# Layer norms of a two-layer decoder: sums by matmul onto every partition, a reciprocal root with a Newton step, and another order of the token parts

## The reference

```python
ALPHA = (2.0 * DEPTH) ** 0.25
def layer_norm(x, g, b):
    mu = jnp.mean(x, axis=-1, keepdims=True)
    var = jnp.mean(jnp.square(x - mu), axis=-1, keepdims=True)
    return (x - mu) * lax.rsqrt(var + EPS) * g + b

for l in range(DEPTH):
    x = layer_norm(ALPHA * x + 0.5 * swiglu(x, ffn1_w_in[l], ffn1_w_out[l]), ...)
    x = layer_norm(ALPHA * x + hybrid_mixer(x, ...), ...)      # RG-LRU | gated linear attention | convolution
    x = layer_norm(ALPHA * x + memory_cross_attn(x, mem, ...), ...)
    x = layer_norm(ALPHA * x + 0.5 * swiglu(x, ffn2_w_in[l], ffn2_w_out[l]), ...)
```

## Time and profile before

| | |
|---|---|
| median of 3 runs | 2443.06 us (2442.2 to 2444.05) |
| profiled execution | 2449.32 us, span 2447.5 us |
| mean granted TensorE clock | 0.959 |
| TensorE busy | 2310.8 us, 94% of the span |
| VectorE, ScalarE, GpSimd busy | 45%, 33%, 42% |
| HBM traffic | 211.5 MB, 86 GB/s |

### The profile page before, as it was taken

One profiled execution on the slowest core, in us unless ns is written; L12 is line 12 of the kernel. 1 busy time (PEld: TensorE's weight loads), 2 busy tenths in 40 slices (PEclk: granted clock), 3 DMA queues, 4 the chain that ended last, 5 costly groups with the idle time before them and its releaser, 6 DMA issues.

```text
span 2447.5 us, 26512 instructions
## 1 busy us (share of the span) xinstructions
PE 2310.8 (94%) x10912; PEld 1920.0 (78%) x10912; DVE 1111.5 (45%) x1179; ACT 797.6 (33%) x1079; POOL 1031.1 (42%) x430
## 2 busy tenths in 40 slices
PE   7999998969999899999999999989799998999997
PEld 6888887856878788888788888877568877888886
DVE  2333325886644533332333332359866454333333
ACT  3322224524444422222233222145345434222222
POOL 5444444423462444444344444343245624444441
PEclk9999998978999899999899999999789998999998
DMA  4223221211341132332122232212113411322321
GB/s 166 95 95 107 101 85 61 86 38 56 97 133 54 55 103 95 99 113 95 64 87 95 95 108 98 79 61 78 48 60 100 129 53 62 101 96 95 112 95 35
DMA packets 55721, 213.24 MB, mean 87 GB/s; under 512 B 6064, under 2 KB 8368, under 8 KB 55344
## 3 DMA queue, kind: packets, MB, share of 16 engines
q1 hardware_dynamic: 54304, 207.64, 25.5%
q10 hardware_dynamic: 1296, 3.90, 0.4%
HBM read 209.42 MB, written 2.10 MB: 86 GB/s over the span
## 4 chain that ended last, share of the span: by engine, by line
PE 82%; DVE 9%; ACT 3%; ACTq 1%; POOL 1%; DVEq 1%; issue 1%; DMA 0%; SPq 0%
PE psum L457 23%; PE psum L458 23%; PE psum L461 23%; DVE tmp L1520 4%; POOL w_lo L380 1%; PE psum L588 1%; PE psum L493 1%; ACT x L1048 1%; PE psum L664 1%; PE psum L620 1%; PE psum L665 1%; ACTq L1062 1%; ACT act_hi L1063 1%; PE psum L670 1%; ACT w_hi L1011 1%
## 5 line engine op out<-in xcount | busy, mean ns | idle before, releaser
L380 POOL TENSOR_TENSOR w_lo<-raw,w_hi 128x1024 fp32r<-128x1024 f32 (+2 forms) x360 | 945.6, 2629 | 1307.8 <-ACT w_hi L1011 1307.7
L1011 ACT ACTIVATE w_hi<-raw 128x1024 fp32r<-128x1024 f32 (+2 forms) x360 | 405.2, 1126 | 1362.5 <-PE psum L461 1237.5
L457 PE MATMUL psum<-act_hi,w_hi 128*128 128x512 f32 x1836 | 728.3, 397 | 36.2 <-ACT w_hi L1011 36.2
L458 PE MATMUL psum<-act_lo,w_hi 128*128 128x512 f32 x1836 | 724.0, 394 | 0.0
L461 PE MATMUL psum<-act_hi,w_lo 128*128 128x512 f32 x1836 | 454.0, 389 | 0.0
L457 PEld LDWEIGHTS psum<-act_hi,w_hi 128*128 128x128 f32 x1836 | 351.0, 191 | 115.9 <-issue 35.5
L458 PEld LDWEIGHTS psum<-act_lo,w_hi 128*128 128x128 f32 x1836 | 350.8, 191 | 73.8 <-issue 0.5
L461 PEld LDWEIGHTS psum<-act_hi,w_lo 128*128 128x128 f32 x1836 | 344.7, 188 | 72.1
L1436 DVE TENSOR_TENSOR work<-work,psum 128x512 f32<-128x512 f32 x88 | 60.5, 688 | 609.5 <-PE psum L461 562.2
L457 PE MATMUL psum<-h_hi,w_hi 128*128 128x512 f32 x616 | 243.3, 395 | 0.0
L458 PE MATMUL psum<-h_lo,w_hi 128*128 128x512 f32 x616 | 243.3, 395 | 0.0
(11 more groups left out here) (246 smaller groups left out, 2410.9 us busy)
## 6 DMA issues: line engine op xcount, KB each, us to landing
raw<-w_in SPq DMA_DIRECT2D x176, 512.0 KB, 3.5
raw<-w_out SPq DMA_DIRECT2D x64, 704.0 KB, 4.0
raw<-w_mix SPq DMA_DIRECT2D x36, 512.0 KB, 3.5
raw<-w_kv SPq DMA_DIRECT2D x32, 512.0 KB, 3.5
raw<-w_mixout SPq DMA_DIRECT2D x16, 576.0 KB, 3.7
raw<-w_q SPq DMA_DIRECT2D x16, 512.0 KB, 3.5
raw<-w_o SPq DMA_DIRECT2D x16, 512.0 KB, 3.5
raw<-w_v SPq DMA_DIRECT2D x4, 768.0 KB, 4.1
```

The costliest lines, as they stand in the source:

```text
L380: nc.gpsimd.tensor_tensor(w_lo[:, n % SPLIT, 0:width], raw[:, n % RAW, 0:width], w_hi[:, n % SPLIT, 0:width].bitcast(F32), ALU.subtract).t ...
L457: nc.tensor.matmul(o, hi, b_hi, start=start and k == 0, stop=False)
L458: nc.tensor.matmul(o, hi, b_lo, start=False, stop=False)
L1011: A(w_hi[:, n % SPLIT, 0:width], raw[:, n % RAW, 0:width], ACT.Copy).then_inc(w_hi_made, 1)
```

## The change

`column_means` turns the sums round: the stationary operand is a 128 x 128 matrix of 1/1024 (one column of `consts`, repeated), the moving one the 256 or 512 tokens, in fp32. Mean and mean square then stand on every partition, in one bank per half (two banks in norm 1). `bcast`, `twice` and the scalar columns go. ScalarE squares the mean into a new tile `var`, VectorE subtracts it from the mean square and clamps (`variance`), ScalarE takes `Abs_reciprocal_sqrt` into `psum`, and VectorE does one Newton step (`scale`): all on 128 x 256 or 128 x 512. The mean is subtracted from `x` before the scale is applied, and where possible before it is known.

```diff
-            def column_sums(n, h, a, source, start, stop):
-
-                t0, t1 = tokens_in(n, h)
-                for t in range(t0, t1):
-                    c = a * (t1 - t0) + t - t0
-                    last = nc.tensor.matmul(psum[:, 6 + h, c:c + 1], source[:, t * P:(t + 1) * P],
-                                            average, start=start and t == t0,
-                                            stop=stop and t == t1 - 1)
+            def column_means(o, sources, cols, start, stop):
+
+                for source in sources:
+                    last = nc.tensor.matmul(o, average, source[:, cols],
+                                            start=start and source is sources[0],
+                                            stop=stop and source is sources[-1])
                 return last
...
                 pe.wait_ge(consts_loaded, 16)
                 pe.wait_ge(z_summed, sum_count(layer, n, min(WHOLE[n], KT - 1) - 1))
-                column_sums(n, h, 0, zsum, True, False)
-                column_sums(n, h, 1, zsqsum, False, False)
+                column_means(mean_of(n, h), [zsum], cols, True, False)
+                column_means(square_mean_of(n, h), [zsqsum], cols, not BY_HALVES[n], False)
...
-                stats_first(layer, n, 0)
-                stats_first(layer, n, 1)
                 hi_ready(layer, s + 1)
                 hi_passes(1, 0, FT // 2, o, a)
                 slot_ready(layer, s + 1)
                 lo_passes(1, o, a).then_inc(half_done, 1)
                 o = psum[:, 3, b]
-                hi_passes(0, 0, 6, o, b)
+                hi_passes(0, 0, 4, o, b)
+                stats_first(layer, n, 0)
                 stats_rest(layer, n, 0)
-                hi_passes(0, 6, FT // 2, o, b)
+                hi_passes(0, 4, FT // 2, o, b)
                 lo_passes(0, o, b).then_inc(slot_multiplied, 1)
-                hi_passes(1, 0, 4, o, b)
-                bcast(layer, n, 0)
-                hi_passes(1, 4, FT // 2, o, b)
+                hi_passes(1, 0, FT // 2, o, b)
+                stats_first(layer, n, 1)
                 lo_passes(1, o, b).then_inc(slot_multiplied, 1)
...
                 stats_rest(layer, 1, 0)
-                k_tile(2)
-                bcast(layer, 1, 0)
-                for m in range(3, KT):
+                for m in range(2, KT):
                     k_tile(m)
...
+                act.wait_ge(stats_ready, group(layer, n, h))
+                A(var[:, tokens_in(n, h)], mean_of(n, h), ACT.Square).then_inc(mean_squared, 1)
+
             def root(layer, n, h):
                 act.wait_ge(var_ready, group(layer, n, h))
-                c, w = SC0[h], 2 if BY_HALVES[n] else 4
-                A(small[:, c + 12:c + 12 + w], small[:, c + 8:c + 8 + w],
-                  ACT.Sqrt).then_inc(std_ready, 1)
+                A(first_root_of(n, h), var[:, tokens_in(n, h)],
+                  ACT.Abs_reciprocal_sqrt).then_inc(root_ready, 1)
...
+                square_of_mean(layer, n, 0)
                 root(layer, n, 0)
                 w_hi_of(next_s)
                 scaled_pair(layer, n, 0, 0)
+                scaled_pair(layer, n, 0, 2)
+                square_b()
                 w_hi_of(next_s + 1)
-                square_b()
-                scaled_pair(layer, n, 0, 2)
+                square_of_mean(layer, n, 1)
+                scaled_pair(layer, n, 0, 4)
                 root(layer, n, 1)
-                silu_table()
-                scaled_pair(layer, n, 0, 4)
                 scaled_pair(layer, n, 0, 6)
                 for k in range(0, KT, 2):
                     scaled_pair(layer, n, 1, k)
+                silu_table()
...
-                sqrt_table()
+                root_table()
                 for m in range(KT):
                     if m == RAW:
                         act.wait_ge(mem_loaded, layer * 16 + 16)
@@ -1252,8 +1240,9 @@
 
                 read_k(0)
                 read_k(1)
+                square_of_mean(layer, 1, 0)
+                read_k(2)
                 root(layer, 1, 0)
-                read_k(2)
...
+            def variance(layer, n, h, eps):
+
+                v = var[:, tokens_in(n, h)]
+                V.tensor_tensor(v, square_mean_of(n, h), v, ALU.subtract)
                 dve.drain()
-                V.tensor_tensor(sq, mean, mean, ALU.mult)
+                V.tensor_scalar(v, v, 0.0, eps, ALU.max, ALU.add).then_inc(var_ready, 1)
+
+            def scale(layer, n, h):
+
+                v, r0 = var[:, tokens_in(n, h)], first_root_of(n, h)
+                dve.wait_ge(root_ready, group(layer, n, h))
+                V.scalar_tensor_tensor(v, v, -0.5, r0, ALU.mult, ALU.mult)
                 dve.drain()
-                V.tensor_tensor(sq, psum[:, 6 + h, w:2 * w], sq, ALU.subtract)
+                V.tensor_tensor(v, v, r0, ALU.mult)
                 dve.drain()
-                V.tensor_scalar(var, sq, 0.0, eps, ALU.max, ALU.add).then_inc(var_ready, 1)
-                dve.wait_ge(std_ready, group(layer, n, h))
-                V.reciprocal(sq, std)
+                V.scalar_tensor_tensor(scale_of(n, h), v, 1.5, r0, ALU.add, ALU.mult)
...
+                    centered(k)
+                scale(layer, n, 0)
+                for k in range(KT):
+                    if k >= KT // 2:
+                        centered(k)
+                    dve.drain()
+                    V.tensor_tensor(x[:, k, :], x[:, k, :], scale_of(n, 0),
+                                    ALU.mult).then_inc(y_centered, 1)
...
             def norm_by_halves(layer, n, eps, added_b):
 
-                scalars(layer, n, 0, eps)
-                centered_pair(layer, n, 0, 0)
-                added_b()
-                centered_pair(layer, n, 0, 2)
-                centered_pair(layer, n, 0, 4)
-                scalars(layer, n, 1, eps)
-                centered_pair(layer, n, 0, 6)
-                for k in range(0, KT, 2):
-                    centered_pair(layer, n, 1, k)
+                for h in range(2):
+                    if h:
+                        added_b()
+                    dve.wait_ge(mean_squared, group(layer, n, h))
+                    variance(layer, n, h, eps)
+                    centered_pair(n, h, 0)
+                    centered_pair(n, h, 2)
+                    scale(layer, n, h)
+                    normed_pair(n, h, 0)
+                    normed_pair(n, h, 2)
+                    for k in range(4, KT, 2):
+                        centered_pair(n, h, k)
+                        normed_pair(n, h, k)
```

The order of the first pair of tiles:

```diff
-                for k in range(2):
-                    hi_by_hi(0, k, a, start=k == 0)
-                slot_ready(layer, s)
-                for k in range(2):
-                    lo_by_hi(0, k, a)
+                for k in range(0, 4, 2):
+                    x_hi(0, k)
+                    for u in range(k, k + 2):
+                        hi_by_hi(0, u, a, start=u == 0)
+                    slot_ready(layer, s)
+                    for u in range(k, k + 2):
+                        lo_by_hi(0, u, a)
                 stats_rest(x_layer, n, 1)
                 hi_ready(layer, s + 1)
-                for k in range(2):
+                for k in range(4):
                     hi_by_hi(1, k, a, start=k == 0)
-                for k in range(2, KT, 2):
-                    if k == KT - 2:
-                        bcast(x_layer, n, 1)
+                for k in range(0, 4, 2):
+                    x_lo(0, k)
+                    for u in range(k, k + 2):
+                        hi_by_lo(0, u, a)
+                        hi_by_lo(1, u, a)
+                for k in range(4, KT, 2):
                     x_hi(0, k)
                     for u in range(k, k + 2):
                         hi_by_hi(0, u, a)
                         lo_by_hi(0, u, a)
                         hi_by_hi(1, u, a)
-                    x_lo(0, k - 2)
-                    for u in range(k - 2, k):
-                        hi_by_lo(0, u, a)
                 slot_ready(layer, s + 1)
                 for k in range(KT):
                     lo_by_hi(1, k, a)
-                x_lo(0, KT - 2)
-                for k in range(KT - 2, KT):
-                    hi_by_lo(0, k, a)
+                for k in range(4, KT, 2):
+                    x_lo(0, k)
+                    for u in range(k, k + 2):
+                        hi_by_lo(0, u, a)
                 for k in range(0, KT, 2):
                     x_hi(1, k)
                     for u in range(k, k + 2):
                         hi_by_hi(0, u, b)
                         lo_by_hi(0, u, b)
                         hi_by_hi(1, u, b)
-                        hi_by_lo(1, u, a)
+                    if k >= 4:
+                        for u in range(k, k + 2):
+                            hi_by_lo(1, u, a)
                     if k:
                         x_lo(1, k - 2)
                         for u in range(k - 2, k):
                             hi_by_lo(0, u, b)
-                for k in range(KT):
```

(83 more changed lines are left out.)

53 lines of the change are left out of this document (31 added, 22 removed).

## The result

The changed kernel takes 2371.95 us (median of 4 runs, 2367.34 to 2374.89) against 2442.63 us before (4 runs): ratio 0.9709, 95% interval 0.9691 to 0.9728. Its profiled execution took 2373.73 us, its span is 2371.9.

The account below looks back on a forecast made before the run. TensorE was taken to stand or crawl around the eight norms. Gains 21.6 + 17.4 + 14.6 + 0 + 2.6 = 56.2 us, less 1.2 x 5 for the clock, gave 50: 2393 us, range 2380 to 2416 (forecast case 2383 to 2404).

Parts of the forecast that it names:

- The block's end: End of four feed-forward blocks: 14.4 us with no stop left and the clock up, a gain of 21.6 us.
- the kernel's end: Last stretch of the kernel: GpSimd idle, so no lock; 14.4 us against 17.0, a gain of 2.6 us.
- The first pair: First pair of tiles behind three feed-forward blocks: 19.1 us against 24.9, 24.8 and 24.6, a gain of 17.4 us.
- The clamp: Variance clamp of half 1 in the pair: waits for GpSimd's weight split, over 2 us, done at 5.3 us.
- The stop for `act_lo`: In the pair: a new TensorE stop of 2.7 us for token pair 2, hidden behind ScalarE's chain.
- Attention: Two norms behind the attention: end 9.2 us, gain 2.6; pair 22.2 us, gain 4.7; together 14.6 us.
- Mixer: Two norms behind the mixer: ScalarE's first affine at the same distance as now, gain 0, between -1 and +2 us.
- The allowance for the clock: Five first pairs: 1.2 us each taken off the gain for a clock that is low part of the time.
- only TensorE's own part pays: Rival: the ends gain 21.6 + 5.2 us but each pair stays as long as now; 2416 us, chance 0.17.
- No lock wait: Rival: the clamp slips ahead of the split and the clock stays up, 8.5 + 6 us more; 2378 us, chance 0.12.
- The kept work was in the way: Denies a rival: ScalarE or weights set the stage behind, so early arrival is waited away; 2443 us, chance 0.03.
- The low clock did not last: Denies a rival: the pair's new stop leaves TensorE at half speed into the 512-column tiles; 2468 us, chance 0.03.

Follow-up runs that it names:

- a_pad32w: The changed kernel with 32 unused words between lam and h_hi, so the region starts 256 past a multiple of 512 as before the change: 2387.02 us.
- b_pad96w: The kernel before with 96 unused words between lam and h_hi, giving the tiles behind them the changed kernel's place modulo 512: 2424.09 us.
- a_all32w: The changed kernel with 32 unused words ahead of x, so that every tile moves by 128 bytes: 2371.58 us.
- a_psum_clamp: The changed kernel with the variance's difference written back to PSUM and the clamp reading it there: 2368.74 us.
- a_psum_clamp_lo: The changed kernel with the clamp reading PSUM, and GpSimd making act_lo of token pair 2 ahead of the second weight split: 2369.29 us.
- b_sums_late: The kernel before with 96 words of padding and its first one-column sums moved to where the change has its sums: 2409.05 us.
- a_sums_early: The changed kernel with the first sums back at their old place behind tile 7's first weight slot: 2384.55 us.

## Why the prediction was wrong

By its own steps, with the stretches above:

- **The block's end: right.** 14.5 and 14.3 us against 14.4 forecast, no stop, clock 1.00. With the kernel's end, the four gained 26.4 us against 24.2 (21.6 + 2.6). The working that expected the clock to stay up once stop and thin records were gone stands, for these ends.
- **The first pair: right in its chain, 0.4 to 0.7 us too long.** 18.7, 18.5 and 18.4 us against 19.1. The gain is 17.5 us by the table and 18.7 with the stops of some 0.5 us before the pairs, which the forecast counted here; it said 17.4 (its own lengths, 24.9, 24.8 and 24.6 less 19.1, give 17.0). The clamp took 1.71 us beside the split and not over 2: it ended 0.15 us behind the split, where the forecast had allowed 0.4, and was done at 5.1 (5.3 forecast). The stop for `act_lo` was 2.5 us (2.7 forecast), the last four pairs came 1.69 us apart (ScalarE):

```profile
387.35 0.63 ACT L1049 ACTIVATE act_hi<-x 128x512 fp32r<-128x512 f32 x1
...
389.03 0.63 ACT L1049 ACTIVATE act_hi<-x 128x512 fp32r<-128x512 f32 x1
```

- **Attention: 12.9 us against 14.6.** Its end took 9.5 us (9.2 forecast), its pair 22.7 against 22.2, since TensorE's clock is low for a while there and the last sums of half 1 run at half speed. How much of the 12.9 is the change's depends on what it is measured from: at the old distance (a_pad32w against before) all of it, at the new one (after against b_pad96w) 9.8, because the padded kernel before has already lost the low clock in its attention ends.
- **Mixer: right.** The first affine comes 17.1 us behind the first key tile's start in both kernels (645.2 to 662.34, 631.1 to 648.24). The 3.9 us in the table are probably not the change's: in the thirteen profiles with `act` at its usual distance the two mixers, whose code is the same but for the table load, take 461 to 470 us, in both families, by where the low clock falls. In a_all32w the first mixer has 10 us less of it than in the kernel after and is 4.4 us shorter; the two spans differ by 6.8 us.
- **The allowance for the clock, 1.2 us in each of five pairs: wrong for three, right for two.** Behind feed-forward blocks the low clock is there (0.91 in the pair), but ScalarE's chain hides it, as a_psum_clamp and a_psum_clamp_lo show. In the attention's pair it costs what was allowed: 21.1 us with 3.4 us of low clock (after), 19.9 without (a_all32w, the same code). With the allowance, the forecast for the attention was 12.2 us against 12.9.
- **The step that failed: the sum held only what the change touches.** It took the duration of every other instruction as given, a term put at nothing without a reason, though the diff resizes `small`, drops `twice` and adds `var` ahead of the tiles that 2,000 matmuls read. That shift is worth 15 us by a_pad32w (2387.02 against 2371.95; 14 in the profiled spans) and 17 us by b_pad96w. With the old distance the changed kernel takes 2387 us, inside the forecast's own range of 2383 to 2404; no rival named it, so the range could not hold it. In the profiled spans 75.6 us were won, 19.4 more than the 56.2 of the sum before its allowance: 13.9 are the pitch in w_out and the attention's output tiles, 3.9 the mixers, 2.2 the ends, 1.0 the rest, and the pairs and the attention together lack 1.6.

The rivals: "only TensorE's own part pays" fell with the pairs' 17.5 us. "No lock wait" gave nearly the right time (2378) for a reason that the 1.71 us clamp refutes, and its price was too high: without the wait (a_psum_clamp) the five pairs win 3.9 us, not 8.5. The kept work was in the way. The low clock did not last: 3.4 us in each pair behind a block.

The 71 us by cause, each run against the kernel before on its own chip: 17 the place in memory (b_pad96w: 2441.17 to 2424.09; 15 when it is taken from the changed kernel), 13 more the place of the sums in the order (b_sums_late: 2439.30 to 2409.05, less 17; a_sums_early gives back 13 too), some 41 the rest, each to about 6 us by the intervals: wide sums and the root chain they allow, the order in half 0, and the load behind the pair. Within the rest only the order of the pair (2 us) and the load (3 us) were taken apart; wide sums and root chain were not.

## What to carry to other kernels

A change that resizes or removes a tile moves all tiles behind it; compare addresses before trusting a difference of under 1%, and pad to tell layout from the edit. Where stages are limited by different engines, compare stretch by stretch: 3 us in a total that scatters by 8 were plain in stretches that repeat within 0.1 us. A stop of an engine costs nothing where another engine's chain ends the stage; and the small VectorE clamp on the critical chain beside GpSimd's work was better off with its operand in PSUM, and 0.13 us worse off where GpSimd was idle.

## What the hardware showed that was not expected

- A 512-column matmul of 4-byte operands starts every 0.2267 us when moving operand and weights lie a multiple of 256 bytes apart, every 0.2289 at 64 bytes off, every 0.2333 (`h_hi`) or 0.2327 (`act_hi`) at 128. Shifting both together changes nothing.
- The 1.45 us stop, and the one-column records, each without the other, left the clock at 1.00 in the block's ends (four of four each); together they were followed by a low clock in ten of twelve. In the attention's end of the kernel before, the records alone were followed by it.
- A VectorE clamp of 256 columns: 0.29 us with GpSimd idle, 1.71 beside its split, 0.42 beside it when the source is in PSUM.
